# Finer waits at four handovers: activations taken chunk by chunk between slabs of a two-layer decoder

## The chip, the cores and the metric

One core of a Trainium2 chip. The metric is the device time of one execution in microseconds (us), lower is better. The engines are TensorE (PE: matmuls, PEld: its weight loads), VectorE (DVE), ScalarE (ACT), GpSimd (POOL) and SyncE (SP, which issues the weight loads by DMA). Each has its own queue and runs it in order; they meet at semaphores.

## The reference

Two layers on 520 tokens (512 of a prompt, 8 single-token samples) of width 1024. Each layer: RMS norm, an input projection to 2824 columns, three mixers side by side (causal pooling, an mLSTM with 4 heads of 128, a gated spatial MLP), an output projection, norm and residual; then an FFN (layer 0 dense SwiGLU with 2816 hidden columns, layer 1 the two best of 8 experts), norm and residual; then a gate from the layer's own embedding.

```
for i in range(DEPTH):
    h = rms(x, norm_mix_pre[i]);  mix = mixers(h @ w_in[i]) @ w_out[i]
    x = x + rms(mix, norm_mix_post[i])
    h = rms(x, norm_ffn_pre[i])
    f = (silu(h @ wg) * (h @ wu)) @ wd        if i == 0 else moe(h)
    x = x + rms(f, norm_ffn_post[i])
    gate = sigmoid(rms(x, norm_ple[i]) @ ple_w_gate[i])
    x = x + gate * (p[i] @ ple_w_proj[i])
```

## The kernel before

All activations are kept transposed: 128 channels on the partitions, 520 tokens along the row. A chunk is such a tile of 128 channels; x, h and y have eight. A projection goes slab by slab: a slab is 128 output columns, that is one weight tile of 128x128 for each input chunk, added up in PSUM (lin, in two pairs of banks that alternate with the slab's parity s). To keep float32 precision, weights and activations are split into a high part (ACT copies it rounded: whi, h_hi, y_hi, gu_hi) and a low part (DVE subtracts: wlo, h_lo, y_lo, gu_lo), and each chunk takes six matmuls of 260 columns: high by high, high by low and low by high, for two halves of the tokens.

Norms are applied late. h is x times the norm's column weights only; the factor of the row (rn) multiplies the slab's result on its way out of PSUM. So h of a chunk needs only x of that chunk, while the squares of x for the factor are added up beside it.

The order of everything is written out by hand, engine by engine, with semaphores that count. For each slab SP loads the weights four slabs ahead (it waits until PE has finished the slab that had the buffer), ACT and DVE split them one pair of slabs ahead, PE multiplies, and DVE (or ACT) takes the result out and raises pair_free. pe_slab counts finished slabs; lo_done counts split ones.

The places that the change touches:

- **w_in to w_out, in both layers.** w_in has 22 slabs; the last four (z 18 to 21) are the output gates, whose sigmoid is made as three ACT passes (Exp, Ln, Exp, L1314 to L1318). y has eight chunks, used in the order Y_ORDER = 0, 1, 6, 7, 2, 3, 4, 5: 0 and 1 come from pooling, 6 and 7 from the spatial MLP, 2 to 5 are the mLSTM heads times their gates. POOL multiplies the first three heads (L598), DVE the last one (`mixers`, step n == 21), and DVE multiplies the eight sample tokens of all four heads at once. The last slab's gate is needed for chunk 5 alone. After all this ACT rounds the eight chunks and DVE makes the eight low parts, and PE starts w_out's first slab chunk by chunk as y_ok counts up. y_hi and y_lo lie on the same memory as h_hi and h_lo, chunk upon chunk, so a chunk of y can be written only when the last w_in slab has read that chunk of h; the wait for the whole last slab covers that.
- **The dense FFN.** It is done in two halves (e = 0, 1) of eleven hidden chunks. Each half has eleven pairs of gate and up slabs and then eight down slabs of eleven chunks each. Before the first down slab PE waits until all eleven chunks gu are split.
- **The gate slabs of layer 0 to w_in of layer 1.** The eight slabs of ple_w_gate read h of that norm; DVE scales each result (into sgs), ACT applies the sigmoid, and `gated` adds it to a chunk of x (ple_x counts). The new h of layer 1 lies where the old one lies. ACT waits for the last gate slab, loads the table for Ln and Exp and rounds eight chunks; DVE, after the last chunk's gate and two adds of squares, makes eight low parts. PE starts layer 1's first w_in slab chunk by chunk by h_ready.

POOL also fills a DRAM buffer (xslot, 5.2 MB) with zeros while layer 0's w_out runs, and then loads p.

Of the kernel before, what the change touches and what calls it, by code (L numbers as in the profile page):

```python
# [23 lines left out]
f32 = mybir.dt.float32  # L24
# [3 lines left out]
ALU = mybir.AluOpType  # L28
# [25 lines left out]
LN_EXP_SET = 6  # L54
Y_ORDER, Y_PARTS = (0, 1, 6, 7, 2, 3, 4, 5), 8
P_AFTER = (4, 6)
CAP = 160
# [33 lines left out]
def build(nc, A, O):  # L91
    ctx = ExitStack()
    with ctx:
# [193 lines left out]
        r_ready = sem("r_ready")  # L287
        h_hi_ok, h_ready = sem("h_hi_ok"), sem("h_ready")
        ut_ready, x_dve, x_pool, ple_x = sem("ut_ready"), sem("x_dve"), sem("x_pool"), sem("ple_x")
# [369 lines left out]
        def _(pe):  # L659
# [36 lines left out]

            def slab(q, par, s, kc, rhs_hi, rhs_lo, order=None, ready=None, out=None):

                ks = range(kc) if order is None else order
                w = 2 * par + s  # L700
                pe.wait_ge(lo_done, q * 2 + (s + 1))
                if out is None:
                    out = lin[:, 2 * s:2 * s + 2]
                    if not (isinstance(q, int) and q == 0):
                        pe.wait_ge(pair_free[s], q)
                for k in ks:
                    whk, wlk = whi[:, w, k * P:(k + 1) * P], wlo[:, w, k * P:(k + 1) * P]
                    st, en = k == ks[0], k == ks[-1]
                    if ready is not None:
                        ready(k)  # L710
                    for a in range(2):
                        o = out[:, a, 0:HALF]
                        mm(o, whk, two(rhs_hi[:, k])[:, a], st, False)
                        mm(o, whk, two(rhs_lo[:, k])[:, a], False, False)
                    for a in range(2):
                        last = mm(out[:, a, 0:HALF], wlk, two(rhs_hi[:, k])[:, a], False, en)
                last.then_inc(pe_slab, 1)

# [164 lines left out]
            for L in range(DEPTH):  # L883
# [11 lines left out]
                for n in range(2 * WIN_P):  # L895
                    q = win_base(L) + n // 2
                    slab(q, q % 2, n % 2, DC, h_hi, h_lo, None, new_h(3 * L, None if L else 0) if n == 0 else None)
                    if n == 0:
                        if L:
                            mean_of_sum(5 * L)  # L900
                        else:
                            mean(0, DC - 1)
                        gates_of()
                    mixers(L, n)
# [154 lines left out]
                else:  # L1059
                    for e in range(SLICES[0]):  # L1060
# [7 lines left out]
                        else:  # L1068
                            stream(b, GU_P, kcs("gu"), (hh, hh))
                        pe.wait_ge(gu_ok, GU_P * (e + 1))  # L1070
                        stream(b + GU_P, DOWN_P, kcs("down"), (gg, gg))
                    mean_of_sum(3, lambda: project_p(0, 0))
# [10 lines left out]
                for n in range(DC):  # L1083
                    q = ple_base(L) + 1 + n // 2
                    slab(q, q % 2, n % 2, DC, h_hi, h_lo, None, gate_ready if n == 0 else None,
                         aux[:, 2:4] if n == 0 else None)
                    if n == 0:
                        mean(5 * L + 4, DC - 1)
# [3 lines left out]
        def _(act):  # L1092
# [79 lines left out]
            def rows_of(c):  # L1172

                act.wait_ge(hx_t, c + 1)
                cp(htok[:, 0:TT, c * P:(c + 1) * P], lin[:, c % 4, :].rearrange("p (t d) -> p t d", d=P)).then_inc(hx_ok, 1)

            def rsqrt(out, in_, eps=True):
# [115 lines left out]
            for L in range(DEPTH):  # L1293
                log_exp_table()
                if L:
                    act.wait_ge(pe_slab, win_base(L) * 2)
                    new_h(3 * L, 8 * L, lambda c: act.wait_ge(ple_x, DC * (L - 1) + c + 1))
                    square(5 * L, DC - 1, two(x[:, DC - 1]))
                else:
                    new_h(0, 0, lambda c: act.wait_ge(x_in[c // 2], 16), 0)  # L1300
                    split(0, 0, 1, DC)
# [6 lines left out]
                for n in range(2 * WIN_P):  # L1308
                    q, s = win_base(L) + n // 2, n % 2
                    split(q + 1, (q + 1) % 2, s, DC)  # L1310
                    mixers(L, n)
                    if n >= Z_O:
                        z_in(act, L, n)
# [5 lines left out]

                act.wait_ge(pool_y, 2 * L + 2)  # L1320
                for k in Y_ORDER:
                    if k == 6:
                        act.wait_ge(g_y, L + 1)
                    if k == 2:
                        act.wait_ge(st_y, L + 1)
                    if 2 <= k < 6:
                        act.wait_ge(hy2, H * L + k - 1)
                    cp(y_hi[:, k], z[:, y_from(k)]).then_inc(y_hi_ok, 1)

# [155 lines left out]
                for n in range(DC):  # L1485
                    q, s = b + 1 + n // 2, n % 2
                    if n < 6 or L < DEPTH - 1:
                        split(q + 1, (q + 1) % 2, s, DC)
                    act.wait_ge(pair_free[s], q + 1)
                    nc.scalar.activation(sgs[:, s], sgs[:, s], ACT.Sigmoid).then_inc(sg_ok, 1)  # L1490
# [3 lines left out]
                if L == 0:  # L1494
                    act.wait_ge(ple_x, DC - 1)
                    square(5, DC - 2, two(x[:, DC - 2]))
# [3 lines left out]
        def _(dve):  # L1500
# [67 lines left out]
            def mixers(L, n):  # L1568
# [85 lines left out]
                if n == 20:  # L1654
# [16 lines left out]
                    for h in range(H):  # L1671
                        last = stt(numS[:, h, :], numS[:, h, :], cols[:, 84 + 4 * L + h:85 + 4 * L + h], sqS[:, h, :], ALU.mult, ALU.mult)
                if n == 21:
                    dve.drain()
                    dve.wait_ge(sig_o, H * (L + 1))
                    tt(z[:, Z_O:Z_O + H, SEQ:TOK], z[:, Z_O:Z_O + H, SEQ:TOK], numS[:, :, :], ALU.mult).then_inc(st_y, 1)
                    dve.wait_ge(hy2, H * L + H - 1)
                    at = z[:, Z_O + H - 1, 0:SEQ]
                    tt(at, z[:, Z_Q + 3 * (H - 1), 0:SEQ], at, ALU.mult).then_inc(hy2, 1)

            split(0, 0, 0, DC)
            dve.wait_ge(cols_in, 16)
            for L in range(DEPTH):
                for c in range(DC):
                    if L == 0:
# [8 lines left out]
                for n in range(2 * WIN_P):  # L1694
                    q, s = win_base(L) + n // 2, n % 2
                    split(q + 1, (q + 1) % 2, s, DC)
                    dve.wait_ge(pe_slab, q * 2 + (s + 1))
                    dve.wait_ge(r_ready, 1 + 5 * L)
                    tt(two(z[:, n]), lin[:, 2 * s:2 * s + 2, 0:HALF], two(rn), ALU.mult).then_inc(pair_free[s], 1)
                    mixers(L, n)  # L1700
                for i, k in enumerate(Y_ORDER):
                    dve.wait_ge(y_hi_ok, Y_PARTS * L + i + 1)
                    tt(y_lo[:, k], z[:, y_from(k)], y_hi[:, k].bitcast(f32), ALU.subtract).then_inc(y_ok, 1)

# [219 lines left out]
                for n in range(DC):  # L1924
                    q, s = b + 1 + n // 2, n % 2
                    if L == 0:
                        add_squares(5, n - 3)
                    dve.wait_ge(pe_slab, q * 2 + s + 1)
                    dve.wait_ge(r_ready, 1 + 5 * L + 4)
                    if n >= 2:  # L1930
                        dve.wait_ge(ple_x, DC * L + n - 1)
                    o = lin[:, 2 * s:2 * s + 2, 0:HALF] if n else aux[:, 2:4, 0:HALF]
                    tt(two(sgs[:, s]), o, two(rn), ALU.mult).then_inc(pair_free[s], 1)
                    if n:
                        gated(n - 1)
# [104 lines left out]
```

## Time and profile before

| what | value |
|---|---|
| runs | 1822.76 us median of 3 (1822.02 to 1825.23) |
| the profiled execution | 1826.82 us, its span 1825.1 us |
| PE busy | 1725.6 us (95%), 12618 matmuls |
| DVE, ACT, POOL busy | 578.8, 472.3, 259.0 us |
| chain that ended last | PE 92%, DVE 3%, ACT 2%, DMA 1%, issue 1% |
| mean granted clock | 0.966 of full speed |

The timeline lists instructions by their start; the number in brackets is how long the engine had been idle before, and who released it. A matmul of 260 columns shows 0.28 us at the full clock and 0.42 at half, but they overlap: the starts of chunks (six matmuls each) tell the pace. "x8" on a row merges eight like instructions that follow one another, with the time from the first start to the last end.

### The profile page before, as it was taken

How to read it: one execution, taken by the hardware profiler on the slowest of the kernel's cores; microseconds unless marked ns; L12 is line 12 of the kernel's file. 1: busy time of each engine (PE TensorE's matmuls, PEld its weight loads, DVE VectorE, ACT ScalarE, POOL GpSimd, SP SyncE). 2: the span in 40 equal slices, each digit the busy share in tenths (PEclk: the TensorE clock that was granted, in tenths of full speed). 3: DMA queues.
4: the chain of work that ended last, by engine and by line, in shares of the span. 5: the costliest groups of instructions: out<-in, count | busy, mean ns of one | idle time of the engine just before them, and what ended most of it. 6: DMA issues, size and time to landing. Idle time of an engine off the chain costs nothing.

```text
span 1825.1 us, 29430 instructions
## 1 busy us (share of the span) xinstructions
PE 1725.6 (95%) x12618; PEld 1622.9 (89%) x12618; DVE 578.8 (32%) x919; ACT 472.3 (26%) x836; POOL 259.0 (14%) x327
## 2 busy tenths in 40 slices
PE   7999998999999998899999889999999999999668
PEld 6877898999999997897788779999999999999658
DVE  3443536443244334643434510110101011010155
ACT  5232544222122225432334410110101001010242
POOL 5642211000000003054310220000000000000220
PEclk9999999999999999999999859999999999999879
DMA  4344361222222222222532348678686776866502
GB/s 163 82 88 114 89 191 59 92 97 90 80 92 92 96 78 86 78 64 94 95 95 82 115 146 265 219 235 261 206 295 212 244 245 211 293 198 199 173 7 92
DMA packets 70230, 260.69 MB, mean 143 GB/s; under 512 B 9848, under 2 KB 10368, under 8 KB 70096
## 3 DMA queue, kind: packets, MB, share of 16 engines
q1 hardware_dynamic: 56736, 219.52, 36.9%
q0 software_dynamic: 13376, 39.45, 8.3%
q8 instruction: 92, 1.51, 0.4%
q14 instruction: 26, 0.21, 0.0%
HBM read 237.20 MB, written 21.96 MB: 142 GB/s over the span
## 4 chain that ended last, share of the span: by engine, by line
PE 92%; DVE 3%; ACT 2%; DMA 1%; issue 1%; POOL 0%; DVEq 0%; ACTq 0%; SPq 0%; POOLq 0%
PE lin L661 78%; PE aux L661 12%; DVE zreg L1502 1%; PE aux L969 1%; DVE h_lo L1505 1%; DVE zreg L1505 1%; PE aux L961 1%; ACT h_hi L1094 0%; DMA yrow<-yslot,idxu 0%; DVE x L1502 0%; PE aux L970 0%; ACT htok L1094 0%; PE aux L960 0%; DMA wreg<-in_w_in_slabs 0%; PE aux L807 0%
## 5 line engine op out<-in xcount | busy, mean ns | idle before, releaser
L661 PE MATMUL lin<-h_hi,whi 128*128 128x260 f32 x1616 | 431.8, 288 | 24.5 <-DVE h_lo L1505 24.5
L661 PE MATMUL lin<-h_lo,whi 128*128 128x260 f32 x1616 | 423.8, 284 | 0.0
L661 PEld LDWEIGHTS lin<-h_hi,whi 128*128 128x128 f32 x1616 | 307.6, 190 | 33.7 <-issue 32.9
L661 PE MATMUL lin<-h_hi,wlo 128*128 128x260 f32 x1616 | 327.4, 284 | 0.0
L661 PE MATMUL lin<-zreg,wreg 128*128 128x160 f32 x2304 | 320.5, 301 | 2.8 <-issue 2.8
L661 PEld LDWEIGHTS lin<-zreg,wreg 128*128 128x128 f32 x2304 | 316.1, 191 | 5.0 <-issue 4.9
L661 PEld LDWEIGHTS lin<-h_lo,whi 128*128 128x128 f32 x1616 | 307.3, 190 | 0.5
L661 PEld LDWEIGHTS lin<-h_hi,wlo 128*128 128x128 f32 x1616 | 250.8, 190 | 0.0
L1502 DVE TENSOR_TENSOR wlo<-wreg,whi 128x1024 fp32r<-128x1024 f32 (+1 forms) x140 | 180.5, 1290 | 99.6 <-ACT whi L1094 99.6
L1094 ACT ACTIVATE whi<-wreg 128x1024 fp32r<-128x1024 f32 (+1 forms) x140 | 151.9, 1090 | 73.9 <-DMA wreg<-in_ffn_w_down 29.9
L661 PE MATMUL lin<-region_b,wreg 128*128 128x160 f32 x1056 | 151.9, 300 | 0.0
L661 PEld LDWEIGHTS lin<-region_b,wreg 128*128 128x128 f32 x1056 | 145.0, 190 | 0.7
L1502 DVE TENSOR_TENSOR region_b<-zreg,lin 128x160 f32<-128x160 f32 x88 | 28.3, 321 | 341.7 <-PE lin L661 341.7
L1388 ACT ACTIVATE zreg<-lin 128x160 f32<-128x160 f32 x88 | 26.7, 303 | 346.7 <-PE lin L661 346.7
L1502 DVE TENSOR_TENSOR zreg<-lin,zreg 128x520 f32<-128x520 f32 x79 | 55.1, 698 | 158.9 <-PE lin L661 152.8
L471 POOL TENSOR_TENSOR x<-x,zreg 128x520 f32<-128x520 f32 x16 | 27.0, 1685 | 549.9 <-DVE zreg L1505 549.9
L661 PE MATMUL lin<-gu_hi,whi 128*128 128x260 f32 x352 | 93.2, 286 | 6.0 <-DVE gu_lo L1502 6.0
L661 PE MATMUL lin<-gu_lo,whi 128*128 128x260 f32 x352 | 92.7, 284 | 0.0
L639 POOL DMA_DIRECT2D yslot<-zreg x8 | 4.5, 561 | 605.1 <-DVE ys L1792 605.1
L661 PE MATMUL lin<-y_hi,whi 128*128 128x260 f32 x256 | 69.6, 292 | 9.0 <-DVE y_lo L1502 9.0
L661 PE MATMUL aux<-zreg,const 128*128 128x260 f32 (+1 forms) x216 | 65.6, 436 | 12.8 <-DVE h_lo L1505 8.8
L661 PEld LDWEIGHTS lin<-gu_hi,whi 128*128 128x128 f32 x352 | 67.3, 191 | 6.4 <-DVE gu_lo L1502 6.4
(277 smaller groups left out, 2245.2 us busy)
## 6 DMA issues: line engine op xcount, KB each, us to landing
wreg<-in_moe_w_gate SPq DMA_DIRECT2D x72, 512.0 KB, 4.3
wreg<-in_moe_w_up SPq DMA_DIRECT2D x72, 512.0 KB, 4.4
wreg<-in_moe_w_down SPq DMA_DIRECT2D x48, 704.0 KB, 5.4
wreg<-in_w_in_slabs SPq DMA_DIRECT2D x44, 512.0 KB, 3.6
wreg<-in_ffn_w_gate SPq DMA_DIRECT2D x22, 512.0 KB, 3.4
wreg<-in_ffn_w_up SPq DMA_DIRECT2D x22, 512.0 KB, 3.3
wreg<-in_ffn_w_down SPq DMA_DIRECT2D x16, 704.0 KB, 3.9
ring_more<-in_moe_w_down SPq DMA_DIRECT2D x16, 704.0 KB, 5.7
```

The costliest lines, as they stand in the source:

```text
L471: pool.tensor_tensor(x[:, c], x[:, c], ut[:, 1], ALU.add).then_inc(x_pool, 1)
L639: pool.dma_start(yslot[e * CAP:e * CAP + P, :], ys0).then_inc(y_stored, 16)
L661: return nc.tensor.matmul(out, lhsT, rhs, start=start, stop=stop)
L961: nc.tensor.transpose(aux[:, k % 2, P:CAP], xs[0:CAP2, 1, k * P:(k + 1) * P], ident[0:CAP2, 0:CAP2]).then_inc(xg_t, 1)
L969: nc.tensor.transpose(aux[:, 2 + d % 2, 0:P], ytb[:, d % 2, 0:P], ident)
L1094: return nc.scalar.activation(out, in_, ACT.Copy, **k)
L1388: nc.scalar.activation(sg2[:, i % 2], lin[:, m % 4, 0:CAP], ACT.Silu).then_inc(act_out, 1)
L1502: return nc.vector.tensor_tensor(out, a, b, op)
L1505: return nc.vector.scalar_tensor_tensor(out=out, in0=a, scalar=s, in1=b, op0=op0, op1=op1)
```

## The change

Four edits, all in the order of work and in what is waited for; the arithmetic is the same. (1) The first down slab of each dense half waits for gu chunk by chunk. (2) In the last w_in slab of both layers and in the last gate slab of layer 0, PE signals a new semaphore h_free after each chunk but the last, so that ACT can overwrite that chunk of h. (3) At the end of w_in ACT rounds chunks 0 and 1 of y by these signals, before the last slab is done, and the other chunks between the three passes of the last gate; DVE makes the low parts of chunks 0 and 1 before it takes the last slab out of PSUM, and the last head's products behind the low part of chunk 3. The sample tokens' product is cut in two: three heads early, the last head late. (4) In the last gate slab of layer 0 ACT rounds layer 1's chunks 0 to 5 as they come free; DVE moves that step's weight split and the gate of chunk 6 ahead, makes six low parts, and only then scales the last gate slab; chunks 6 and 7 follow as x comes.

```diff
+FREED_WIN, FREED_PLE = (0, 2 * DC - 2), DC - 1
 PE, slab():
+                    if frees and not en:
+                        last.then_inc(h_free, 1)
 PE, w_in slabs:
-                    slab(q, q % 2, n % 2, DC, h_hi, h_lo, None, new_h(3 * L, None if L else 0) if n == 0 else None)
+                    slab(q, q % 2, n % 2, DC, h_hi, h_lo, None, new_h(3 * L, None if L else 0) if n == 0 else None,
+                         frees=n == 2 * WIN_P - 1)
 PE, dense FFN:
-                        pe.wait_ge(gu_ok, GU_P * (e + 1))
-                        stream(b + GU_P, DOWN_P, kcs("down"), (gg, gg))
+                        stream(b + GU_P, DOWN_P, kcs("down"), (gg, gg), ready=lambda k: pe.wait_ge(gu_ok, GU_P * e + k + 1))
 PE, gate slabs:
-                         aux[:, 2:4] if n == 0 else None)
+                         aux[:, 2:4] if n == 0 else None, L == 0 and n == DC - 1)
 ACT:
+            def round_y(k):
+                cp(y_hi[:, k], z[:, y_from(k)]).then_inc(y_hi_ok, 1)
+            def round_next(c):
+                act.wait_ge(ple_x, c + 1)
+                cp(h_hi[:, c], x[:, c], scale=cols[:, 8 + c:9 + c]).then_inc(h_hi_ok, 1)
 ACT, start of layer 1:
-                    act.wait_ge(pe_slab, win_base(L) * 2)
-                    new_h(3 * L, 8 * L, lambda c: act.wait_ge(ple_x, DC * (L - 1) + c + 1))
+                    round_next(DC - 1)
 ACT, w_in steps:
+                    if n == 2 * WIN_P - 1:
+                        act.wait_ge(pool_y, 2 * L + 2)
+                        for k in (0, 1):
+                            act.wait_ge(h_free, FREED_WIN[L] + k + 1)
+                            round_y(k)
+                        act.wait_ge(pe_slab, win_base(L) * 2 + n + 1)
+                        act.wait_ge(g_y, L + 1)
+                        round_y(6)
+                        round_y(7)
+                        z_in(act, L, n)
+                        nc.scalar.activation(z[:, n], z[:, n], ACT.Exp, scale=-1.0)
+                        act.wait_ge(st_y, 2 * L + 1)
+                        act.wait_ge(hy2, H * L + 1)
+                        round_y(2)
+                        act.drain()
+                        nc.scalar.activation(z[:, n], z[:, n], ACT.Ln, bias=one)
+                        act.wait_ge(hy2, H * L + 2)
+                        round_y(3)
+                        act.drain()
+                        nc.scalar.activation(z[:, n], z[:, n], ACT.Exp, scale=-1.0).then_inc(sig_o, 1)
...
-                act.wait_ge(pool_y, 2 * L + 2)
-                for k in Y_ORDER:
...
+                act.wait_ge(hy2, H * L + 3)
+                round_y(4)
+                act.wait_ge(st_y, 2 * L + 2)
+                act.wait_ge(hy2, H * L + 4)
+                round_y(5)
 ACT, gate steps:
+                    if L == 0 and n == DC - 1:
+                        for c in range(DC - 2):
+                            act.wait_ge(h_free, FREED_PLE + c + 1)
+                            round_next(c)
...
-                    act.wait_ge(ple_x, DC - 1)
+                    round_next(DC - 2)
                     square(5, DC - 2, two(x[:, DC - 2]))
 DVE:
+            def rest_of_y(L, i):
+                k = Y_ORDER[i]
+                dve.wait_ge(y_hi_ok, Y_PARTS * L + i + 1)
+                tt(y_lo[:, k], z[:, y_from(k)], y_hi[:, k].bitcast(f32), ALU.subtract).then_inc(y_ok, 1)
 DVE, w_in steps:
                     split(q + 1, (q + 1) % 2, s, DC)
+                    if n == 2 * WIN_P - 1:
+                        dve.drain()
+                        dve.wait_ge(sig_o, H * L + H - 1)
+                        tt(z[:, Z_O:Z_O + H - 1, SEQ:TOK], z[:, Z_O:Z_O + H - 1, SEQ:TOK], numS[:, 0:H - 1, :], ALU.mult).then_inc(st_y, 1)
+                        for i in range(2):
+                            rest_of_y(L, i)
                     dve.wait_ge(pe_slab, q * 2 + (s + 1))
...
+                for i in range(2, Y_PARTS - 2):
+                    rest_of_y(L, i)
+                dve.wait_ge(sig_o, H * (L + 1))
+                tt(z[:, n, SEQ:TOK], z[:, n, SEQ:TOK], numS[:, H - 1, :], ALU.mult).then_inc(st_y, 1)
+                dve.wait_ge(hy2, H * L + H - 1)
+                tt(z[:, n, 0:SEQ], z[:, Z_Q + 3 * (H - 1), 0:SEQ], z[:, n, 0:SEQ], ALU.mult).then_inc(hy2, 1)
+                for i in range(Y_PARTS - 2, Y_PARTS):
+                    rest_of_y(L, i)
 DVE, gate steps:
+                    if L == 0 and n == DC - 1:
+                        split(q + 1, (q + 1) % 2, s, DC)
+                        gated(n - 1)
+                        for c in range(DC - 2):
+                            low_h(3, 8, c)
                     dve.wait_ge(pe_slab, q * 2 + s + 1)
...
                     tt(two(sgs[:, s]), o, two(rn), ALU.mult).then_inc(pair_free[s], 1)
+                    if L == 0 and n == DC - 1:
+                        low_h(3, 8, DC - 2)
+                        break
```

## Rows read from the trace of the kernel before

**Rows 1.** Waits of PE: engine, line, who released it: us in total, times, longest

```profile
PE lin L661 <- DVE h_lo L1505: 24.5, 3, 12.2
...
PE lin L661 <- DVE y_lo L1502: 9.0, 2, 4.5
PE lin L661 <- DVE gu_lo L1502: 6.0, 2, 3.0
```

**Rows 2.** Timeline of PE, w_out's first slab, layer 0: start, us, line, operation, idle

```profile
227.70 0.56 PE L661 MATMUL lin<-y_hi,whi 128*128 128x260 f32 x1 [4.49 <-DVE y_lo L1502]
...
229.13 0.42 PE L661 MATMUL lin<-y_hi,whi 128*128 128x260 f32 x1
...
230.43 0.42 PE L661 MATMUL lin<-y_hi,whi 128*128 128x260 f32 x1
...
235.95 0.28 PE L661 MATMUL lin<-y_hi,whi 128*128 128x260 f32 x1
```

**Rows 3.** Timeline of PE, w_out's first slab, layer 1

```profile
972.75 0.56 PE L661 MATMUL lin<-y_hi,whi 128*128 128x260 f32 x1 [4.49 <-DVE y_lo L1502]
...
979.84 0.28 PE L661 MATMUL lin<-y_hi,whi 128*128 128x260 f32 x1
...
980.56 0.28 PE L661 MATMUL lin<-y_hi,whi 128*128 128x260 f32 x1
```

**Rows 4.** Timeline of DVE between w_in and w_out, layer 0

```profile
221.09 1.21 DVE L1502 TENSOR_TENSOR wlo<-wreg,whi 128x1024 fp32r<-128x1024 f32 x1
223.25 0.70 DVE L1502 TENSOR_TENSOR zreg<-lin,zreg 128x520 f32<-128x520 f32 x1 [0.96 <-PE lin L661]
...
226.86 4.96 DVE L1502 TENSOR_TENSOR y_lo<-zreg,y_hi 128x520 fp32r<-128x520 f32 x8
```

**Rows 5.** Timeline of ACT between w_in and w_out, layer 0

```profile
223.98 0.64 ACT L1314 ACTIVATE zreg<-zreg 128x520 f32<-128x520 f32 x1 [4.76 <-DVE zreg L1502]
...
226.03 4.31 ACT L1094 ACTIVATE y_hi<-zreg 128x520 fp32r<-128x520 f32 x8
```

**Rows 6.** Timeline of PE, the first down slab of each dense half

```profile
422.27 0.39 PE L661 MATMUL lin<-gu_hi,whi 128*128 128x260 f32 x1 [2.98 <-DVE gu_lo L1502]
...
615.46 0.59 PE L661 MATMUL lin<-gu_hi,whi 128*128 128x260 f32 x1 [2.98 <-DVE gu_lo L1502]
```

**Rows 7.** Timeline of DVE, evacuations of the first down slabs of both halves

```profile
430.53 0.70 DVE L1896 COPY zreg<-lin 128x520 f32<-128x520 f32 x1 [6.77 <-PE lin L661]
...
438.44 0.70 DVE L1896 COPY zreg<-lin 128x520 f32<-128x520 f32 x1 [5.69 <-PE lin L661]
...
625.16 0.70 DVE L1502 TENSOR_TENSOR zreg<-zreg,lin 128x520 f32<-128x520 f32 x1 [8.22 <-PE lin L661]
```

**Rows 8.** Timeline of PE, layer 1's first w_in slab and what follows it

```profile
765.39 0.55 PE L661 MATMUL lin<-h_hi,whi 128*128 128x260 f32 x1 [6.87 <-DVE h_lo L1505]
...
772.80 1.92 PE L661 MATMUL aux<-zreg,const 128*128 128x260 f32 x8
```

**Rows 9.** Timeline of DVE from layer 0's last gate slabs to layer 1's h

```profile
754.80 1.22 DVE L1502 TENSOR_TENSOR wlo<-wreg,whi 128x1024 fp32r<-128x1024 f32 x1
...
764.49 5.45 DVE L1505 SCALAR_TENSOR_TENSOR h_lo<-x,cols,h_hi 128x520 fp32r<-128x520 f32 x8
```

**Rows 10.** Timeline of ACT at the same place

```profile
761.33 1.28 ACT L1136 ACT_TABLE_LOAD   x1
```

**Rows 11.** Two windows: busy us (instructions) of PE, PEld, DVE, ACT, POOL; PEclk, DMA, GB/s

```profile
700.00:715.00 15.00, 9.70 (x61) 8.44 (x60) 7.31 (x11) 7.13 (x13) 5.07 (x4) 1.00 0.11 35
1056.00:1080.00 24.00, 24.00 (x75) 19.09 (x74) 1.15 (x3) 2.58 (x5) 9.28 (x10) 0.50 0.47 178
```

**Rows 12.** DMA from 234 to 238: packets, MB, share; an issue, KB, us to landing

```profile
q0 software_dynamic: 287, 1.04, 96.9%
...
wreg<-in_w_out SPq DMA_DIRECT2D x1, 512.0 KB, 9.3
```

**Rows 13.** DMA issue from 230.6 to 234: KB, us to landing

```profile
zreg<-in_p_t POOLq DMA_DIRECT2D x1, 520.0 KB, 17.4
```

More of the change, by code:

```diff
@@ L287, in build @@
         r_ready = sem("r_ready")
-        h_hi_ok, h_ready = sem("h_hi_ok"), sem("h_ready")
+        h_hi_ok, h_ready, h_free = sem("h_hi_ok"), sem("h_ready"), sem("h_free")
         ut_ready, x_dve, x_pool, ple_x = sem("ut_ready"), sem("x_dve"), sem("x_pool"), sem("ple_x")
@@ L695, in new_h, with slab @@
                 return ready
-            def slab(q, par, s, kc, rhs_hi, rhs_lo, order=None, ready=None, out=None):
+            def slab(q, par, s, kc, rhs_hi, rhs_lo, order=None, ready=None, out=None, frees=False):
                 ks = range(kc) if order is None else order
@@ L1311, in _ @@
                     mixers(L, n)
-                    if n >= Z_O:
+                    if n == 2 * WIN_P - 1:
[18 more added lines that the diff above has]
+                        nc.scalar.activation(z[:, n], z[:, n], ACT.Exp, scale=-1.0).then_inc(sig_o, 1)
+                    elif n >= Z_O:
                         z_in(act, L, n)
@@ L1318, in _ @@
                         nc.scalar.activation(z[:, n], z[:, n], ACT.Exp, scale=-1.0).then_inc(sig_o, 1)
-                act.wait_ge(pool_y, 2 * L + 2)
-                for k in Y_ORDER:
[L1322 to L1328, printed above, removed]
+                act.wait_ge(hy2, H * L + 3)
[3 more added lines that the diff above has]
+                round_y(5)
                 def take_wout(s, q, i):
@@ L1672, in mixers @@
                         last = stt(numS[:, h, :], numS[:, h, :], cols[:, 84 + 4 * L + h:85 + 4 * L + h], sqS[:, h, :], ALU.mult, ALU.mult)
[L1673 to L1679, printed above, removed]
+            def rest_of_y(L, i):
+                k = Y_ORDER[i]
+                dve.wait_ge(y_hi_ok, Y_PARTS * L + i + 1)
+                tt(y_lo[:, k], z[:, y_from(k)], y_hi[:, k].bitcast(f32), ALU.subtract).then_inc(y_ok, 1)
             split(0, 0, 0, DC)
@@ L1683, in _ @@
             for L in range(DEPTH):
-                for c in range(DC):
+                for c in range(0 if L == 0 else DC - 1, DC):
                     if L == 0:
@@ L1700, in _ @@
                     mixers(L, n)
-                for i, k in enumerate(Y_ORDER):
-                    dve.wait_ge(y_hi_ok, Y_PARTS * L + i + 1)
-                    tt(y_lo[:, k], z[:, y_from(k)], y_hi[:, k].bitcast(f32), ALU.subtract).then_inc(y_ok, 1)
+                for i in range(2, Y_PARTS - 2):
[6 more added lines that the diff above has]
+                    rest_of_y(L, i)
                 def lo_of_p(s, q, i):
```

## The prediction, on record before the changed kernel ran

> **What bounds the kernel now.** I read the waits of TensorE first, since PE is busy for 95% of the span. The reader is to see that the waits on h_lo (three, 24.5 us), y_lo (two, 9.0 us) and gu_lo (two, 6.0 us) are handovers: the next slab's first chunk waits for an activation that another engine has just made [rows 1]. Five of them are the change's: y_lo at w_out of both layers, gu_lo at both halves of the dense down projection, and one h_lo (6.87 us [rows 8]) at layer 1's w_in. The other two h_lo waits it doesn't touch. Then I read PE's timeline behind each stall, because a stall also costs clock: behind the 4.49 us stall chunks start 1.30 us apart (229.13, 230.43), while the last chunk of layer 1's first w_out slab takes 0.72 [rows 2, 3]. So I measure each handover from the end of the slab before to the start (or evacuation) of the slab after, which holds both losses. Everywhere else PE runs on, so what a handover saves moves all behind it forward.
>
> **w_out, both layers.** The last w_in slab ends at 227.70 - 4.49 = 223.21, and w_out's second slab starts at 235.95: 12.74 us [rows 2]. In layer 1 it is 972.75 - 4.49 = 968.26 to 980.56: 12.30 [rows 3]. New schedule, in layer 0's times. DVE's split of that step (221.09, 1.21) ends at 222.30 [rows 4]; the sample product follows (24 columns; I leave 0.17 for it, an estimate), then y_lo of chunks 0 and 1 at a pitch of 4.96/8, about 0.61: 223.16 and 223.77 [rows 4]. Their y_hi are no obstacle: ACT idles 4.76 us before 223.98 and two copies take about 1.1 (4.31/8 each) [rows 5]; the chunks of h under them are released after 0.72 and 1.44 us of a slab that starts 5.76 us before 223.21. DVE's product for z[21] (223.25 before) thus comes at 223.69, 0.45 later, and ends at 224.39 [rows 4]. Meanwhile ACT copies chunks 6 and 7 (223.25 to 224.40), then Exp to 225.06, y_hi 2 to 225.59, Ln to 226.39, y_hi 3 to 226.92, last Exp to 227.63, y_hi 4 to 228.16; Exp takes 0.64 [rows 5]. DVE: y_lo 6 at 225.00, 7 at 225.61, 2 at 226.31, 3 at 227.64; the last head's products to 228.40; y_lo 4 at 229.01. y_hi 5 waits for that product and ends at 229.05, y_lo 5 at 229.77. PE starts a chunk 0.14 after its y_lo. With chunks of 0.72 it stalls about 0.4 before chunk 6, 0.5 before 3 and 0.65 before 4, starts the last at 229.89 and the second slab at 230.61. That is 7.40 us, so 5.3 are saved in layer 0 and 4.9 in layer 1: **10.2**. About 2.85 of each is idle time, the rest is clock that isn't lost. The low end, every chunk at 1.30, is 3.0 less for a slab: 2.3 and 1.9. I take the high one: the largest new gap is 0.65, and there is a stretch with larger gaps at the full clock (below).
>
> **Dense down, both halves.** Ten of its eleven gu chunks are long ready, and the eleventh is ready where PE starts today, 422.27 and 615.46 [rows 6]. PE reaches it ten chunks, 7.2 us, after 419.29, so after 426.5, and nothing waits. Slabs are evacuated every 7.91 us (430.53, 438.44) [rows 7]. Without the stall the first would be at 419.29 + 7.91 = 427.2 and 612.48 + 7.91 = 620.4 in place of 430.53 and 625.16 [rows 6, 7]: 3.3 and 4.8, together **8.1**. The second is larger, since the clock fell there and not in the first. Ends: 6.0 (the idle times alone) and 9.5 (if in most executions it falls at both). Late next is the second slab's low weight half, written by DVE right behind gu_lo: ready near 423.8 where PE now needs it at 427.2, so 3.4 us of cover are left.
>
> **Layer 1's first w_in slab.** PE ends the gate slab at 765.39 - 6.87 = 758.52 and goes on behind the w_in slab at 772.80 [rows 8]. DVE now moves its last split ahead (1.22, after an add of 0.69 behind the split that ends at 756.02: to 757.8), then the gate of chunk 6 (two passes of 0.70 [rows 7], to 759.15), then six h_lo at 5.45/8, about 0.67 [rows 9]: 759.83 to 763.18. PE starts at 759.97 and does six chunks by 764.29. Only then comes the last gate's product (to 763.8), which waited at 758.55 before: this is what queues behind the moved h_lo. Sigmoid to 764.5, a square to 765.0, h_hi 6 to 765.6, h_lo 6 at 766.4: PE stalls 2.3. The gate of chunk 7 to 767.8, two adds to 769.0, h_lo 7 at 769.7: PE stalls 2.6, does chunk 7 and goes on at 770.56. The table load (1.28) [rows 10] ends at 767.5, ahead of the gate, and costs nothing; if it came after, 1.28. So 2.24 are saved at the full clock. But PE works 0.72 of 5.55 us there, so I expect the clock to fall. The nearest row is the second down slab: 2.98 idle cost 4.8 - 3.3 = 1.5 behind it [rows 6, 7]. That leaves **0.7**. Ends: 2.2 with no loss, and -0.3 with what the first w_out slab lost (235.95 - 227.70 less eight chunks of 0.72: 2.5).
>
> **Waits and signals on PE.** 22 waits and 21 signals are added inside slabs. Layer 1's first w_out slab has such a wait at each chunk, and its last chunk (979.84 to 980.56) takes 0.72, as 7.91/11 does without [rows 3, 7]. I take 0. The other end is a matmul's tail laid bare at each: 0.28 less 0.12 = 0.16, times 43: 6.9. Below nothing is excluded, since they replace no work.
>
> **Sum.** 10.2 + 8.1 + 0.7 = 19.0 us. The profiled execution took 1826.82 (span 1825.1), so 1807.8. It lies 4.1 over the median of the runs, 1822.76; the same 19.0 off that gives **1803.8**.
>
> **Clock: row and rule.** In the 15 us from 700 PE was busy 9.70, so idle for 5.3, and the granted clock was 1.00; in the 24 us from 1056 PE was busy throughout and had 0.50 [rows 11]. So gaps don't always bring 1.2 GHz, and busy time doesn't always hold 2.4 GHz. The Trainium skill, "TensorE: Matmul & The Clock Gate", section "A second HAM failure mode: psum-queue depth-cycling", says that short idles between groups of matmuls can make the clock swing between its levels. By it the new short gaps at w_out would cost clock too and the sum would be the first rival's; by the stretch from 700 it is 19.0.
>
> **Loads of w_out.** POOL's zero-fill of xslot runs at fixed times in layer 0. The fifth w_out load, issued when the first slab ends, took 9.3 us, and in 234 to 238 the software queue took 96.9% of the engines [rows 12]. It is now issued at 230.6, lands near 240 by that row, and is split some 2.4 us later, against a need at 247.9: nothing is lost. The Trainium skill, "DMA: Bandwidth & Descriptors", section "Queues, rings and completion order", says each DMA engine takes turns between queues; by it the load would land sooner still, and the second rival were out. The row disagrees, so that rival stays.
>
> **Rivals.**
> 1. The clock falls in both w_out slabs in spite of short gaps: 6.0 less saved, so 13.0, and 1809.8. For it: rows 2 after 4.49; against it: the stretch from 700.
> 2. The zero-fill keeps the fifth load out until its queue is empty, with the p load issued at about 232.1 that took 17.4 [rows 13]: 249.5, plus 1.9 to move 0.5 MB at that stretch's 1.04 MB in 4 us [rows 12], plus 2.5 for the splits: 253.9, so PE stalls 6.0: 13.0 saved, 1809.8. Against it: before, the load landed at 245.3, ahead of that.
> 3. The change doesn't do what it says: chunk releases don't come before the slab's end. Then y_hi 0 starts at 223.25, z[21] on DVE moves behind two y_lo, and the last y_lo comes near 231.2: 1.5 less in each w_out, 16.0 saved, 1806.8. Against it: nothing in the trace shows a late signal.
> 4. Slower: the clock doesn't come back after the handovers, as from 1056 to 1080. A chunk at 1.30 costs 0.58; from 33 more chunks (about four slabs) at the low level the 19.0 are gone. Over the eight w_out slabs of one layer it is 64 x 0.58 = 37: 1841. Against it: each of the four falls here cost at most 2.5 us, 4.3 chunks' worth [rows 2, 3, 7, 8].
>
> **Chances.** Forecast 0.66, rivals in order 0.12, 0.05, 0.12 and 0.03, and 0.02 that gains hide in something unseen. Under 0.2% (3.6 us) can't be told from no change. Forecast and the first three rivals are all faster: 0.95; same 0.02; slower 0.03. The range takes the high ends of the handovers (9.5, 10.2 and 2.2, with 2 us for the spread of the runs shown: 1799) and the first two rivals with some of the signals' price (1811).
>
> **What would show it.** Right: no stall of PE before gu_hi's first matmul; w_out's first slab done about 7.4 us after w_in's last, with gaps under 1 us and matmuls at 0.28; two stalls of 2 to 3 us before chunks 6 and 7 of layer 1's w_in. Wrong: w_out chunks 1.30 apart, a wait for wlo at w_out's fifth slab, a chunk pitch over 0.72 in the slabs with signals, or a gap at w_in that is one piece.

## The result and the profile after

The changed kernel took 1809.84 us (median of 4 runs, 1808.82 to 1810.67); the kernel before, in the runs beside it, 1823.99 (4 runs, 1822.02 to 1826.23). The ratio is 0.9918, with 0.9905 to 0.9930 as its interval: 15.0 us faster by the ratio (14.2 between the medians) where 19.0 were forecast, and inside the range given. The changed kernel's profiled execution took 1810.67, its span 1808.9.

The waits of PE, kernel after (columns as in [rows 1]):

```profile
PE lin L662 <- DVE h_lo L1536: 23.6, 5, 12.3
...
PE lin L662 <- DVE y_lo L1533: 1.3, 4, 0.4
```

The row for gu_lo (6.0) is gone and y_lo fell from 9.0 to 1.3. One h_lo wait became three, and their total only from 24.5 to 23.6.

Timeline of PE, kernel after, w_out's first slab of layer 0 and then of layer 1 (chunks 0, 1 and 6, the first three, wait too briefly to get a bracket):

```profile
222.87 0.36 PE L662 MATMUL lin<-y_hi,whi 128*128 128x260 f32 x1
...
224.61 0.39 PE L662 MATMUL lin<-y_hi,whi 128*128 128x260 f32 x1
...
227.28 0.39 PE L662 MATMUL lin<-y_hi,whi 128*128 128x260 f32 x1 [0.26 <-DVE y_lo L1533]
...
228.68 0.39 PE L662 MATMUL lin<-y_hi,whi 128*128 128x260 f32 x1 [0.40 <-DVE y_lo L1533]
...
230.34 0.28 PE L662 MATMUL lin<-y_hi,whi 128*128 128x260 f32 x1
...
961.62 0.39 PE L662 MATMUL lin<-y_hi,whi 128*128 128x260 f32 x1 [0.26 <-DVE y_lo L1533]
...
963.01 0.39 PE L662 MATMUL lin<-y_hi,whi 128*128 128x260 f32 x1 [0.42 <-DVE y_lo L1533]
...
964.68 0.28 PE L662 MATMUL lin<-y_hi,whi 128*128 128x260 f32 x1
```

The slab takes 230.34 - 222.87 = 7.47 us from its first matmul, where it took 8.25 behind an idle 4.49 [rows 2]. The engines that feed it, kernel after, DVE and then ACT; DVE's "x2" is y_lo of chunks 0 and 1, now ahead of z[21]'s product (223.25), which was first before [rows 4]. ACT's two "x2" are y_hi of chunks 0 and 1 (218.67, four us before the last w_in slab ends at 222.76) and of chunks 6 and 7:

```profile
222.03 1.30 DVE L1533 TENSOR_TENSOR y_lo<-zreg,y_hi 128x520 fp32r<-128x520 f32 x2
223.25 0.69 DVE L1533 TENSOR_TENSOR zreg<-lin,zreg 128x520 f32<-128x520 f32 x1
223.86 2.02 DVE L1533 TENSOR_TENSOR y_lo<-zreg,y_hi 128x520 fp32r<-128x520 f32 x3
```

```profile
218.67 1.15 ACT L1098 ACTIVATE y_hi<-zreg 128x520 fp32r<-128x520 f32 x2
222.79 1.17 ACT L1098 ACTIVATE y_hi<-zreg 128x520 fp32r<-128x520 f32 x2 [2.97 <-PE lin L662]
223.98 0.64 ACT L1333 ACTIVATE zreg<-zreg 128x520 f32<-128x520 f32 x1
...
239.84 1.06 ACT L1098 ACTIVATE whi<-wreg 128x1024 fp32r<-128x1024 f32 x1 [2.43 <-DMA wreg<-in_w_out]
```

ACT's eight copies in a row [rows 5] are now cut up by Exp and Ln. The last row is the split of the fifth w_out load: it landed at 239.8 ("near 240" was forecast), and PE waits for no weights there. That load in the DMA view of 230.2 to 231.5, kernel after:

```profile
wreg<-in_w_out SPq DMA_DIRECT2D x1, 512.0 KB, 9.3
```

That is as long as it took before [rows 12].

Evacuations of the first down slabs on DVE, kernel after: 422.44 and 430.36 are the first two of the first half (430.53 and 438.44 before [rows 7]), 612.37 is the second half's first (625.16).

```profile
422.44 0.70 DVE L1936 COPY zreg<-lin 128x520 f32<-128x520 f32 x1 [3.50 <-PE lin L662]
...
430.36 0.70 DVE L1936 COPY zreg<-lin 128x520 f32<-128x520 f32 x1 [5.69 <-PE lin L662]
...
612.37 0.70 DVE L1533 TENSOR_TENSOR zreg<-zreg,lin 128x520 f32<-128x520 f32 x1 [3.50 <-PE lin L662]
```

Layer 1's first w_in slab, PE, then DVE and ACT at the same place, kernel after:

```profile
747.18 0.36 PE L662 MATMUL lin<-h_hi,whi 128*128 128x260 f32 x1 [1.46 <-DVE h_lo L1536]
...
753.66 0.39 PE L662 MATMUL lin<-h_hi,whi 128*128 128x260 f32 x1 [1.93 <-DVE h_lo L1536]
...
757.14 0.59 PE L662 MATMUL lin<-h_hi,whi 128*128 128x260 f32 x1 [2.49 <-DVE h_lo L1536]
...
758.61 3.41 PE L662 MATMUL aux<-zreg,const 128*128 128x260 f32 x8
```

```profile
746.28 4.11 DVE L1536 SCALAR_TENSOR_TENSOR h_lo<-x,cols,h_hi 128x520 fp32r<-128x520 f32 x6
750.31 0.69 DVE L1533 TENSOR_TENSOR zreg<-lin,zreg 128x520 f32<-128x520 f32 x1
...
752.85 0.76 DVE L1536 SCALAR_TENSOR_TENSOR h_lo<-x,cols,h_hi 128x520 fp32r<-128x520 f32 x1 [1.85 <-ACT h_hi L1098]
```

```profile
753.36 1.28 ACT L1140 ACT_TABLE_LOAD   x1
```

The 6.87 of [rows 8] became 1.46, 1.93 and 2.49. The last gate's product (750.31) stands behind six h_lo, and all of chunk 6's h waits for it through ACT. The table load has no wait of PE behind it. From the end of the gate slab (745.72) to the matmuls of the mean (758.61) it is 12.89 where it was 14.28 [rows 8]; but these eight take 3.41 in place of 1.92, so nothing is left.

Each handover by one measure: time between starts of the same PE matmuls, ahead of it and behind it, the mean of two profiled executions of either kernel (the second ones are experiments below).

| stretch | before | after | difference |
|---|---|---|---|
| w_out, layer 0 | 18.65 | 13.61 | -5.04 |
| w_out, layer 1 | 18.34 | 13.62 | -4.72 |
| first down slab, half 1 | 16.71 | 13.45 | -3.26 |
| first down slab, half 2 | 21.49 | 16.81 | -4.68 |
| layer 1's first w_in slab | 21.76 | 21.85 | +0.09 |
| first slab behind layer 0's mixers (FFN, not edited) | 22.20 | 23.05 | +0.85 |
| layer 1's w_in and mixers (not edited) | 187.87 | 189.42 | +1.55 |
| layer 1's router (not edited) | 109.55 | 110.10 | +0.55 |

The edited five give 17.6 back, the three below take 3.0; all other stretches together are 0.4 longer. Unrounded that leaves 14.3, the difference of the mean spans (1823.0 and 1808.7).

### The profile page after: what moved, and what is told of

It reads as the page before. It is cut to its first block, busy times and chain, and to the rows that moved or that the text cites. A ratio compares the mean times of both kernels' runs of the same rounds, so it can differ in the third digit from the quotient of the medians.

```text
span 1808.9 us, 29442 instructions
## 1 busy us (share of the span) xinstructions
PE 1722.9 (95%) x12618; PEld 1619.7 (90%) x12618; DVE 579.6 (32%) x921; ACT 473.2 (26%) x836; POOL 258.1 (14%) x327
## 4 chain that ended last, share of the span: by engine, by line
PE 91%; DVE 4%; ACT 2%; DMA 1%; issue 1%; POOL 0%; ACTq 0%; DVEq 0%; SPq 0%; POOLq 0%
PE lin L662 77%; PE aux L662 12%; DVE h_lo L1536 1%; DVE zreg L1533 1%; PE aux L974 1%; DVE zreg L1536 1%; PE aux L966 1%; ACT h_hi L1098 1%; DMA yrow<-yslot,idxu 0%; DVE x L1533 0%; PE aux L975 0%; ACT htok L1098 0%; PE aux L965 0%; DMA wreg<-in_w_in_slabs 0%; DVE wlo L1533 0%
## 5 line engine op out<-in xcount | busy, mean ns | idle before, releaser
L662 PE MATMUL lin<-h_hi,whi 128*128 128x260 f32 x1616 | 432.8, 289 | 23.6 <-DVE h_lo L1536 23.6
L1098 ACT ACTIVATE zreg<-aux 128x128 f32<-128x128 f32 (+1 forms) x40 | 13.7, 342 | 224.4 <-PE aux L975 112.8
L662 PE MATMUL lin<-zreg,ring_more 128*128 128x160 f32 x512 | 72.2, 299 | 0.0
```

What stands on the lines that cost most here:

```text
L662: return nc.tensor.matmul(out, lhsT, rhs, start=start, stop=stop)
L1098: return nc.scalar.activation(out, in_, ACT.Copy, **k)
```

## The experiments

Ratios are against the kernel before, with their 95% intervals.

**Each part alone.** The first of these kernels has the w_out part, the second the dense part, the third the gate-to-w_in part. The w_out part against the changed kernel (core):

```diff
-FREED_WIN, FREED_PLE = (0, 2 * DC - 2), DC - 1
+FREED_WIN, FREED_PLE = (0, DC - 1), DC - 1
...
+                        pe.wait_ge(gu_ok, GU_P * (e + 1))
...
-                    if L == 0 and n == DC - 1:
-                        split(q + 1, (q + 1) % 2, s, DC)
-                        gated(n - 1)
-                        for c in range(DC - 2):
-                            low_h(3, 8, c)
```

> Only the two handovers to w_out as changed. Theory (the gaps stay short, so the clock stays at its higher level): from the end of w_in to w_out's second slab about 7.5 us in place of 12.74 and 12.30, so 5.2 and 4.8, together 10.0 us less. Rival (the clock falls there all the same): chunks 1.30 apart, 2.3 and 1.9 less, together 4.2 us.

Measured: 1818.15, 0.9966 (0.9953 to 0.9978), 6.2 us off. At the sites it gave all that the whole change gives (13.62 and 13.63), but the first half's down slab behind it took 17.99 where it took 16.71 before, and FFN's first slab 0.86 more.

The dense part against the kernel before:

```diff
-                        pe.wait_ge(gu_ok, GU_P * (e + 1))
-                        stream(b + GU_P, DOWN_P, kcs("down"), (gg, gg))
+                        stream(b + GU_P, DOWN_P, kcs("down"), (gg, gg), ready=lambda k: pe.wait_ge(gu_ok, GU_P * e + k + 1))
```

> Only the chunk-wise wait of the first down slab in both dense halves. Theory: no idle time before gu_hi's first matmul, 3.0 us of idle gone at each half and 1.5 of clock at each half where it fell before: 6.0 to 9.5 us less, 8.1 by the profiled execution before. Rival (the low weight half of the second slab, or waits inside the slab, take its place): a wait for wlo at the second slab or a chunk pitch over 0.72 us, and under 5 us less.

Measured: 1818.56, 0.9968 (0.9955 to 0.9980), 5.8 us off. The two down slabs took 13.45 and 16.81, as with the whole change; layer 1's mixers gave back 1.5.

The gate-to-w_in part against the kernel before (core):

```diff
+FREED_WIN, FREED_PLE = (0, DC - 1), 0
...
+                    if L == 0 and n == DC - 1:
+                        for c in range(DC - 2):
+                            act.wait_ge(h_free, FREED_PLE + c + 1)
+                            round_next(c)
...
+                    if L == 0 and n == DC - 1:
+                        split(q + 1, (q + 1) % 2, s, DC)
+                        gated(n - 1)
+                        for c in range(DC - 2):
+                            low_h(3, 8, c)
```

> Only the handover from layer 0's gate slabs to layer 1's w_in as changed. From PE's end of the last gate slab to its first matmul of the gate weights it was 15.84 us before and 15.94 with all edits. Theory (the two stalls before chunks 6 and 7 bring the clock down again and it costs 2 us after them): again 15.5 to 16.0, so within 0.4 us of before. Rival (the 0.1 us was the phase of one execution, and the handover saves the 2.2 us of the sum at the full clock): 13.6.

Measured: 1825.91, 1.0009 (1.0000 to 1.0018): no gain. The stretch took 21.88 (21.76 before). The three sum to 10.4, less than the whole change's 15.0. Each kernel loses some clock in stretches that it doesn't edit, and this needn't add up; but each of the three figures is uncertain by some 2 us either way, so the gap of 4.6 isn't firm.

**Does w_in's loss lie in the stalls' clock?** Against the changed kernel, this one puts 14 and 18 matmuls of weights by weights, whose result nothing reads, in front of the waits for chunks 6 and 7:

```diff
+                    if N == 3 and k >= DC - 2:
+                        w = 2 * (win_base(1) % 2)
+                        for i in range((14, 18)[k - (DC - 2)]):
+                            mm(aux[:, 2, 0:HALF], whi[:, w, 0:P], whi[:, w, 0:HALF], True, True)
```

> All edits, and PE does idle work in its stalls before chunks 6 and 7 of layer 1's first w_in slab: 14 and 18 matmuls of weights by weights into an unused bank (no result uses them). Theory (the handover saves nothing because the stalls bring the clock down for what follows): no stretch of 1.2 GHz behind chunk 7, and the 15.9 us from the last gate slab to the gate weights become 13.7 to 14.0. Rival (what follows waits for DVE and ACT in any case): 15.9 stays.

Measured: 1808.70, 0.9914 (0.9898 to 0.9931). First the granted clock behind the stalls, kernel after (columns as in [rows 11]), then PE with the idle work:

```profile
751.00:754.80 3.80, 1.73 (x13) 1.31 (x11) 1.88 (x4) 3.59 (x5) 0.00 (x0) 1.00 0.00 0
754.80:761.60 6.80, 4.46 (x13) 3.83 (x14) 2.65 (x5) 1.67 (x3) 0.00 (x0) 0.50 0.21 72
```

```profile
750.75 1.83 PE L662 MATMUL aux<-whi 128*128 128x260 f32 x14
752.85 0.39 PE L662 MATMUL lin<-h_hi,whi 128*128 128x260 f32 x1 [0.27 <-DVE h_lo L1540]
...
753.67 2.30 PE L662 MATMUL aux<-whi 128*128 128x260 f32 x18
756.32 0.39 PE L662 MATMUL lin<-h_hi,whi 128*128 128x260 f32 x1 [0.36 <-DVE h_lo L1540]
...
757.15 1.91 PE L662 MATMUL aux<-zreg,const 128*128 128x260 f32 x8
```

The real chunks wait just as long for their h, yet the mean takes 1.91 and the stretch falls by 2.1 (15.94 to 13.80, end of the gate slab to the first matmul behind the mean). The loss was clock (the granted clock was 1.00 from 750 to 762 in that kernel). Its size can be read from the window: PE was busy for 4.46 at 0.50, and half of that, 2.2, is what the full clock would have saved.

**And w_out's gain?** The same filler (34 matmuls) in the kernel before, in each 4.49 us wait of w_out:

```diff
+                    if k == Y_ORDER[0]:
+                        for i in range(34):
+                            mm(lin[:, 0, 0:HALF], whi[:, w, 0:P], whi[:, w, 0:HALF], True, True)
```

> The kernel before, with 34 such matmuls of idle work in PE's 4.49 us wait ahead of w_out's first slab in both layers; no wait is moved. Theory (about half of what w_out's handover gains is clock): no stretch of 1.2 GHz behind the wait, so 2.5 us less in layer 0 and 2.0 in layer 1, from w_in's end to w_out's second slab about 10.3 us in place of 12.74 and 12.30. Rival (the 1.30 us chunks come from y_lo and DVE, not from the clock): 12.74 and 12.30 stay.

Timeline of PE at layer 0's w_out, the kernel before with the idle work:

```profile
221.33 4.20 PE L661 MATMUL lin<-whi 128*128 128x260 f32 x34
225.90 0.39 PE L661 MATMUL lin<-y_hi,whi 128*128 128x260 f32 x1 [0.37 <-DVE y_lo L1507]
```

The stretch from w_in's end to w_out's second slab fell from 12.74 (12.50 in the second profile of before) to 10.25, in layer 1 from 12.30 to 10.25. So of the change's 5.0 and 4.7 about half was clock and half idle time, as the prediction had it. The whole kernel: 1823.27, 0.9991 (0.9980 to 1.0002), not clearly different: 2.4 + 2.05 were saved, the first down slab, where the clock now fell too, gave back 2.7 (19.42 for 16.71), and FFN's first slab and layer 1's w_in handover 0.7 and 0.6.

**Do waits and signals on PE cost anything?** The changed kernel with a signal and an already fulfilled wait at the chunks of all slabs (965 more signals and 1051 more waits on PE in its trace):

```diff
+                    else:
+                        pe.wait_ge(c_in, 16)
...
+                    elif not en:
+                        last.then_inc(h_more, 1)
```

> All edits, and a signal after each chunk and a wait that is long fulfilled ahead of each chunk in every slab of w_in, w_out, the dense FFN and the gates, some 950 of each where the change adds 21 and 22. Theory (they cost nothing on PE): a chunk pitch of 0.72 us, and within 2 us of the change. Rival (a tail of 0.16 us laid bare at each, the other end of the price in the prediction): some 150 us more, chunks 0.88 us apart.

Measured: 1808.30, 0.9915 (0.9899 to 0.9932), within the interval of the change alone. First matmul of each of two chunks in w_out, that kernel:

```profile
239.45 0.29 PE L662 MATMUL lin<-y_hi,whi 128*128 128x260 f32 x1
...
240.17 0.28 PE L662 MATMUL lin<-y_hi,whi 128*128 128x260 f32 x1
```

0.72 apart, as without. The price of zero holds; at the other end, 0.16 each, it would have been some 150 us.

**What are the early releases worth at w_out?** y of chunks 0 and 1 waits for the whole last w_in slab again, all else as changed:

```diff
-                            act.wait_ge(h_free, FREED_WIN[L] + k + 1)
+                            act.wait_ge(pe_slab, win_base(L) * 2 + n + 1)
```

> All edits, but y of chunks 0 and 1 waits for the whole last w_in slab in place of the two chunk signals; orders stay. Theory (the early copies take DVE's low parts of chunks 0 and 1 off the path): from w_in's end to w_out's second slab 9.1 us in place of 7.6 in both layers. Rival (the interleaved order alone makes the gain, the signals none): 7.6 stays.

One run: 1812.79, which says little by itself, since its profile lost 3.1 in layer 0's mixers, ahead of every edit (177.9 from 42 to 217, where both profiles of before and after have 174.8). PE at layer 0's w_out, that kernel:

```profile
226.80 0.36 PE L662 MATMUL lin<-y_hi,whi 128*128 128x260 f32 x1 [1.61 <-DVE y_lo L1533]
...
231.20 0.39 PE L662 MATMUL lin<-y_hi,whi 128*128 128x260 f32 x1 [0.26 <-DVE y_lo L1533]
...
232.60 0.39 PE L662 MATMUL lin<-y_hi,whi 128*128 128x260 f32 x1 [0.42 <-DVE y_lo L1533]
```

Both stretches are 1.50 longer than with the change (15.11, 15.12), the third rival's own price. So with the new order of the work alone w_out gains 3.5 and 3.2, and freeing h early adds 1.5 in each layer.

**Why did two profiles of before and after differ elsewhere?** Both kernels once more, with no edit.

> The kernel before once more, unchanged, for a second profile. Question: the four handovers gave 17.6 us in the trace and about 15 in the times. Theory (the clock that a handover loses differs between executions, and the profiled one was a slow one): the same idle times (4.49, 2.98, 2.98, 6.87, 4.49), but from w_in's end to w_out's second slab and over the first down slabs lengths that differ by up to 1.7 us from 12.74, 12.30, 11.2 and 12.6. Rival (the lengths are fixed and the edits cost something elsewhere): the same lengths within 0.2 us.

> The changed kernel once more, unchanged, for a closer interval and a second profile. Theory: 14 to 16 us less than before; w_out's handovers 7.6 us, no idle time at the down slabs, layer 1's w_in handover 15.5 to 16.0 as in the first profile; low-clock stretches at other places than there in the mixers, 1.5 us each. Rival: the handovers differ from the first profile by over 0.3 us.

Measured: 1822.61 (one run) and 1809.70, 0.9917 (0.9904 to 0.9931). My theory, that the same handover differs by up to 1.7 us from one execution to the next, fell: before's five handovers lie within 0.25 of the first profile, after's within 0.05. The slow stretch in layer 1's mixers, expected at other places, came at the same one (915.2 and 915.5). The two profiles of before differ by 4.2 in span, and most of that lies behind 1700 (118.70 against 115.98), where PE waits in long gaps anyway, and in the first 217 us (0.9).

**Taking w_in's loss out by order.** DVE computes three h_lo, the last gate's product, gate 6, three h_lo, gate 7, two h_lo, then the splits, so that chunks 6 and 7 aren't late:

```diff
-                        split(q + 1, (q + 1) % 2, s, DC)
-                        gated(n - 1)
-                        for c in range(DC - 2):
+                        for c in range(3):
                             low_h(3, 8, c)
...
-                        low_h(3, 8, DC - 2)
+                        gated(n - 1)
+                        for c in range(3, DC - 2):
+                            low_h(3, 8, c)
+                        gated(n)
+                        for c in range(DC - 2, DC):
+                            low_h(3, 8, c)
```

> All edits, and the last gate slab's order on DVE changed: three h_lo, then the last gate's product, the gate of chunk 6, three h_lo, the gate of chunk 7, the last two h_lo, and the weight split behind all of it. Theory (the stalls before chunks 6 and 7 come from the six h_lo ahead of the last gate's product): gaps of about 0.9 us before chunk 3 and 1.3 before chunk 6 in place of 1.5, 1.9 and 2.5, the clock stays up, and the stretch from the last gate slab to the gate weights takes about 10 us in place of 15.9: 6 us less than with the change alone, about 21 less than before. Rival (DVE's total work sets the end of the stretch, wherever the product stands): chunk 7 no earlier, under 1 us less than the change alone.

Measured: 1804.79, 0.9891 (0.9876 to 0.9906), 5 under the change. PE at layer 1's w_in, that kernel:

```profile
750.64 0.39 PE L662 MATMUL lin<-h_hi,whi 128*128 128x260 f32 x1 [0.68 <-DVE h_lo L1536]
...
754.04 0.39 PE L662 MATMUL lin<-h_hi,whi 128*128 128x260 f32 x1 [0.97 <-DVE h_lo L1536]
...
756.34 2.02 PE L662 MATMUL aux<-zreg,const 128*128 128x260 f32 x8 [0.42 <-DVE zreg L1533]
```

The stretch fell from 21.85 to 16.12, 5.6 under the kernel before. In this order the finer handover pays at w_in; with the change's order on DVE it didn't. What this order would give without the chunk signals wasn't run.

**Best version.** That kernel with 41 idle matmuls in each of two waits of 5.4 us that no edit touches, ahead of FFN's first slab and of layer 1's first gate slab:

```diff
+                    if k == 0 and N in (1, 4):
+                        o = lin[:, 0, 0:HALF] if N == 1 else aux[:, 2, 0:HALF]
+                        for i in range(41):
+                            mm(o, whi[:, w, 0:P], whi[:, w, 0:HALF], True, True)
```

> gate_first, and 41 matmuls of idle work (weights by weights, no result uses them) in each of two waits of about 5.4 us that the change leaves alone: ahead of the dense FFN's first slab and ahead of layer 1's first gate slab. Theory (idle work keeps the clock up across a wait): no 1.2 GHz stretch behind these two, 1.5 to 2.8 us less at each, so 3 to 5.5 us less than gate_first. Rival (the wait's end moves out, since the idle matmuls hold something up): no gain.

Measured: 1803.77, 0.9880 (0.9865 to 0.9895), the lowest median, but only 1.0 under the kernel without filler, where 3 to 5.5 were expected, and with intervals that overlap. FFN's stretch fell by 1.84 (22.82 to 20.98); at the gate slab nothing came (35.06 to 35.10). The granted clock of that gate slab, kernel with the idle work:

```profile
1739.00:1746.00 7.00, 5.32 (x31) 4.58 (x31) 6.20 (x10) 3.28 (x6) 2.11 (x2) 1.00 0.00 0
```

The clock was held there as well (it was 0.54 without, from 1740.5 to 1747), but PE is busy for only 5.32 of the 7.00 and DVE for 6.20, and from 1733 to 1747 PE waits three times for DVE's h_lo, 1.9 us in all (without the idle work there was the one wait of 5.4): the slab goes at DVE's pace, so the faster PE gains nothing.

## Why the prediction was right, and what was off

The total was in the range and on the right side; 6.0 lie between 1803.8 and 1809.84. Of these 1.2 are the base (1822.76 in three runs, 1823.99 in the four beside the change), 4.8 the gain: 19.0 forecast, 14.2 between the medians. By the table 1.4 of the 4.8 are in the terms of the sum, 3.0 in stretches that no term covers, and 0.4 in the rest. That the range reaches down to such a gain is luck: its slow end stands on the first two rivals, both of which also give 1809.8, and neither of them happened. The total alone would have pointed to them; the trace rules them out.

- **w_out, 10.2:** measured 5.04 + 4.72 = 9.8. The stalls were 0.26 and 0.40 where 0.5 and 0.65 stood, and the clock didn't fall, so the first rival is out. The granted clock of the slab, kernel after:

```profile
222.80:230.30 7.50, 6.71 (x48) 6.05 (x49) 6.42 (x11) 6.34 (x10) 7.50 (x9) 1.00 0.94 290
```

 By the Trainium skill, "TensorE: Matmul & The Clock Gate", section "A second HAM failure mode: psum-queue depth-cycling", frequent short idles let the clock swing; here, with gaps of 0.26 and 0.40, it stayed at 1.00.
- **Dense down, 8.1:** 3.26 + 4.68 = 7.9. No wait took the place of the old one.
- **w_in, 0.7:** measured -0.1, and this is the term that was mis-sized, though inside its ends. The three pieces came as worked out (PE's start 1.45 after the slab and stalls of 2.3 and 2.6 forecast; 1.46, 1.93 and 2.49 measured). Its 2.24 at the full clock was right (2.05 with the idle work: 15.85 before, 13.80). Its clock loss of 1.5, taken from the second down slab, was 2.1. Half the time that PE is busy in the stretch at 0.50 sizes it better.
- **Waits and signals, 0:** right, as the thousand more of each show.
- **Loads:** the second rival is out by the split at 239.84. The prediction took [rows 12] to speak against queues taking turns; that was a misreading. The load's packets start 5 us late and then take their turns (last section). The third is out by the rows of DVE (y_lo 0 started at 222.03, before the slab's end at 222.76), and its price was right. The fourth is out: each fall of the clock that a handover brought ended within the next slab or so.
- **What no step had:** 3.0 lost in stretches without an edit. At FFN's first slab the wait is as long as before (5.45 and 5.46), but the clock fell later in it. First the kernel before, then after:

```profile
280.80:287.60 6.80, 3.98 (x15) 3.78 (x16) 5.13 (x8) 3.87 (x7) 3.35 (x2) 0.50 0.01 2
```

```profile
276.80:283.70 6.90, 5.66 (x22) 5.30 (x23) 5.82 (x9) 4.32 (x8) 2.22 (x2) 0.51 0.01 2
```

 Before, PE was busy for 3.98 of the slow stretch, after for 5.66: half of the difference is 0.84, and 0.85 was measured. So that loss is accounted for. Why the fall comes later isn't: it came 2.4 to 2.9 us into the wait in both profiles of before, in the dense part, in the gate-to-w_in part and in the kernel without early releases, and 3.5 to 4.4 us into it in the others that show it. The kernel without early releases has every other edit and still took no longer there than before (22.2), so it isn't the edits as such.

 In layer 1's mixers PE had no wait at all; the clock stayed up in both profiles of before and fell in both of after. The same work before, then after; the first row of each is the 10 us ahead:

```profile
918.00:928.00 10.00, 10.00 (x58) 6.08 (x57) 2.05 (x3) 1.71 (x3) 0.00 (x0) 1.00 0.31 105
928.00:931.00 3.00, 3.00 (x27) 3.00 (x27) 1.81 (x4) 1.38 (x4) 1.62 (x3) 1.00 0.07 22
```

```profile
905.00:915.20 10.20, 10.20 (x60) 6.28 (x59) 2.06 (x3) 1.71 (x3) 0.00 (x0) 1.00 0.34 103
915.20:918.60 3.40, 3.40 (x18) 3.40 (x18) 1.81 (x4) 1.38 (x4) 1.61 (x3) 0.50 0.09 24
```

 The rows ahead are alike, the clock behind isn't: half of 3.40 is 1.7, and 1.55 was measured. That stretch was 1.5 to 2.1 longer in both profiles of after, in both part kernels without the w_out part, in the one with the extra signals, the one without early releases and both reordered ones, and 3.0 longer with w_in filled (two falls); not in the two profiles of before, nor in the kernel before with w_out filled, nor with the w_out part alone. But such falls aren't the change's own. Layer 0's mixers, which lie ahead of all four edits, show one in eleven of the thirteen profiles and three in the other two. This is one in the second profile of before:

```profile
180.40:183.80 3.40, 3.40 (x18) 3.40 (x18) 1.81 (x4) 1.38 (x4) 1.62 (x3) 0.50 0.09 24
```

 It is the same work in layer 0, with the same busy times. So whether the change brings the fall in layer 1's mixers isn't shown; what decides it stays open, as does the router's 0.55.

## What to carry to other kernels

Price a handover as its idle time plus half of the time that the matrix engine is busy in the slow stretch behind it, and read both from a window of the granted clock. Cutting one wait into three saves little if the pieces still let the clock fall: look for what queues between the pieces on the producing engine (here a gate product behind six h_lo) before adding finer signals, which cost nothing measurable here. Hold some of the forecast back for slow stretches that come, go and move elsewhere (3.0 of 17.6 here, the cause open).

## What the runs showed of the hardware that was not expected

- A full engine didn't hold the clock: in the kernel after it fell from 1.00 to 0.50 at 915.2 with PE busy for 10.20 of the 10.20 us ahead. The last of that work were these, one column wide, and two of 32 columns:

```profile
913.22 1.84 PE L662 MATMUL aux<-zreg,region_b 128*128 128x1 f32 x16
```

 That isn't the cause by itself: behind the same work it stayed at 1.00 in the kernel before (928 to 931), and in layer 0 of that kernel it fell at 127.3 behind matmuls of 128 to 512 columns, with PE busy for 10.20 of 10.20 there too.
- Idle matmuls in a wait of 4.5 to 5.5 us held the clock at 1.00 at all four places where they stood in such a wait (both w_out, FFN, the gate slab); time was gained at three. In the kernel with w_out filled the clock fell later, at the first down slab's wait (0.50 from 418.0 to 424.8), where it had stayed up before; it did so with the w_out part alone, too (from 416.9), so the idle work isn't shown to have brought that.
- Beside the transfers on the software queue (the zero-fill, then p), w_out's fifth load, issued at 230.54 on the hardware queue, moved nothing for 5 us: its first packet started at 235.7. From 236 to 238 both had the same share of the engines. The DMA view of 232 to 234 (with no row of the hardware queue), then of 236 to 238, kernel after:

```profile
q0 software_dynamic: 150, 0.54, 100.2%
```

```profile
q1 hardware_dynamic: 100, 0.41, 49.9%
q0 software_dynamic: 100, 0.36, 49.9%
```

 The Trainium skill, "DMA: Bandwidth & Descriptors", section "Queues, rings and completion order", has each engine take turns between its queues; the second view agrees. What kept the load from starting isn't shown.
